# Splitting the picks' softmax, and the order of hits and high parts in the last retrieval head of a PEER block on one Trainium2 core

## The reference, cut to what matters

```
q = (xt @ w_query).reshape(T, PEER_HEADS, 2, D_HALF)
s = jnp.einsum('thpd,hpnd->thpn', q, sub_keys)
top_s, top_i = lax.top_k(s, PEER_TOPK)
cand = (top_s[:, :, 0, :, None] + top_s[:, :, 1, None, :]).reshape(T, PEER_HEADS, PEER_TOPK * PEER_TOPK)
best_s, best_c = lax.top_k(cand, PEER_TOPK)
i1 = jnp.take_along_axis(top_i[:, :, 0], best_c // PEER_TOPK, axis=-1)
i2 = jnp.take_along_axis(top_i[:, :, 1], best_c % PEER_TOPK, axis=-1)
ids = i1 * N_KEYS + i2
gates = jax.nn.softmax(best_s, axis=-1)
y[t] = sum_k gelu(expert_down[ids[t, k]] . x[t]) * gates[t, k] * expert_up[ids[t, k]]
```

## Time and profile before

| what | value |
|---|---|
| median of 3 runs | 1507.16 us (1506.37 to 1509.75) |
| the profiled execution, its own time | 1509.32 us |
| its span in the profile | 1507.5 us |
| mean granted TensorE clock | 0.993 |
| PE busy | 1453.1 us, 96% |
| DVE, ACT, POOL busy | 1162.8, 626.2 and 576.9 us |

### The profile page before, as it was taken

The page is one execution under the profiler, slowest core; times in us unless marked ns, Lnnn a source line. Parts: engine busy times, 40 slices in busy tenths (PEclk is TensorE's granted clock), DMA queues, the critical chain, the costliest instruction groups (busy, mean ns, idle before and its releaser), DMA issues.

```text
span 1507.5 us, 21376 instructions
## 1 busy us (share of the span) xinstructions
PE 1453.1 (96%) x7494; PEld 1252.9 (83%) x7494; DVE 1162.8 (77%) x2434; ACT 626.2 (42%) x985; POOL 576.9 (38%) x460
## 2 busy tenths in 40 slices
PE   3999999999999989999999999999999999999997
PEld 3455548999999889999988888888888888888886
DVE  6557565667888978988757787878778788888887
ACT  3134434344544357776633333333333333333334
POOL 0000011136444356888923343334334344444340
PEclk9999999999999999999999999999999999999999
DMA  9944303546464457787799999999999999999993
GB/s 350 387 176 168 99 28 119 156 140 228 132 204 168 127 177 255 266 286 266 256 377 372 336 341 360 351 336 340 362 331 358 344 362 340 339 383 348 331 334 108
DMA packets 186554, 404.89 MB, mean 269 GB/s; under 512 B 13064, under 2 KB 100688, under 8 KB 184784
## 3 DMA queue, kind: packets, MB, share of 16 engines
q1 hardware_dynamic: 146864, 243.86, 46.1%
q0 software_dynamic: 36864, 134.23, 24.2%
q10 hardware_dynamic: 2720, 25.44, 4.6%
HBM read 360.49 MB, written 42.99 MB: 268 GB/s over the span
## 4 chain that ended last, share of the span: by engine, by line
PE 87%; DVE 5%; POOL 3%; ACT 2%; issue 2%; DMA 2%; SPq 0%; POOLq 0%; ACTq 0%; DVEq 0%
PE bank L1838 11%; PE bank L1839 11%; PE bank L1840 11%; PE bank L1765 10%; PE bank L1767 10%; PE bank L1766 10%; PE bank L1820 4%; PE bank L1662 4%; PE bank L1707 3%; PE bank L1734 2%; PE bank L1735 2%; PE bank L1733 2%; PE bank L1646 2%; POOL gated L727 2%; PE bank L1755 1%
## 5 line engine op out<-in xcount | busy, mean ns | idle before, releaser
L1765 PE MATMUL bank<-h2hi,dhi 128*128 128x384 f32 x1024 | 348.1, 340 | 11.5 <-DVE dlo L1264 10.2
L1767 PE MATMUL bank<-h2hi,dlo 128*128 128x384 f32 x1024 | 344.7, 337 | 0.0
L1766 PE MATMUL bank<-h2lo,dhi 128*128 128x384 f32 x1024 | 344.3, 336 | 0.0
L1838 PE MATMUL bank<-uhi,ahi 128*128 128x512 f32 x768 | 299.6, 390 | 2.4 <-DVE alo L1489 2.4
L1264 DVE TENSOR_TENSOR dlo<-down,dhi 128x1024 fp32r<-128x1024 f32 x128 | 164.9, 1289 | 174.6 <-ACT dhi L856 167.5
L1839 PE MATMUL bank<-ulo,ahi 128*128 128x512 f32 x768 | 299.3, 390 | 0.0
L1840 PE MATMUL bank<-uhi,alo 128*128 128x512 f32 x768 | 299.2, 390 | 0.0
L680 POOL DMA_INDIRECT rows<-in_peer_up,ids x128 | 162.7, 1271 | 237.3 <-DVE y L1341 207.2
L680 POOL DMA_INDIRECT rows<-in_peer_down,ids x128 | 160.6, 1255 | 216.2 <-DVE rows L1332 197.4
L856 ACT ACTIVATE dhi<-down 128x1024 fp32r<-128x1024 f32 x128 | 135.1, 1056 | 216.3 <-PE bank L1767 208.7
L1765 PEld LDWEIGHTS bank<-h2hi,dhi 128*128 128x128 f32 x1024 | 193.4, 189 | 16.2 <-DVE dlo L1264 13.3
(11 more groups left out here) (201 smaller groups left out, 1935.2 us busy)
## 6 DMA issues: line engine op xcount, KB each, us to landing
down<-in_down_t SPq DMA_DIRECT2D x128, 512.0 KB
up<-in_peer_up SPq DMA_DIRECT2D x128, 512.0 KB
ada<-in_w_ada SPq DMA_DIRECT2D x48, 512.0 KB, 11.3
gate<-gates_dram SPq DMA_DIRECT2D x32, 768.0 KB, 9.1
gates_dram<-stage ACTq DMA_DIRECT2D x11, 2048.0 KB, 7.1
gel_dram<-gel SPq DMA_DIRECT2D x80, 192.0 KB
gelu<-gel_dram SPq DMA_DIRECT2D x80, 192.0 KB
wq<-in_peer_query SPq DMA_DIRECT2D x16, 512.0 KB, 5.3
```

What stands on the lines that cost most here:

```text
L1765: pe.matmul(bank[7 * s][:, 0:TD], dhi[s][:, k, :], h2hi[:, k, 0:TD], start=k == 0, stop=False)
L1766: pe.matmul(bank[7 * s][:, 0:TD], dhi[s][:, k, :], h2lo[:, k, 0:TD], start=False, stop=False)
L1767: last = pe.matmul(bank[7 * s][:, 0:TD], dlo[s][:, k, :], h2hi[:, k, 0:TD], start=False, stop=k == KT - 1)
L1838: pe.matmul(got[:], ahi[j][:, tokens], uhi[j][:, half], start=first, stop=False)
```

## The change

It does four things.

1. The softmax's subtraction and Exp are done in two parts: heads 0 to 6 (VectorE before the last head's `top16`, ScalarE right behind the last scores' copies), and head 7 alone (VectorE right behind `picks_of(7)`, ahead of low 46; ScalarE where Exp stood). `best_exp` is the new function on ScalarE, `best_sub` on VectorE.
2. ScalarE's hits of head 7 are cut into halves: half 0, then high 47 and Gelu 45, then half 1, then high 48 and Gelu 46.
3. GpSimd waits for `dve_half` of the last head before `weigh_hits(6)`, that is until the last head's sums are written.
4. VectorE does low 49 ahead of `select(7)` and not behind the numbers; low 50 comes ahead of the three row operations, low 51 behind hot rows 0, and low 52 stays behind hot rows 1.

```
@@ gpsimd
+            gp.wait_ge(dve_half, PH)
             for s in range(2):
                 weigh_hits(PH - 2, s)
             measure_hits(PH - 1)
@@ scalar
+            def hits_of(h, s):
+
+                flat = hit[s][:].rearrange("p b i j -> p (b i j)")
+                act.wait_ge(pool_off, 2 * h + s + 1)
+                act.activation(flat, flat, ACT.Abs).then_inc(act_far, 1)
+                act.wait_ge(act_far, 2 * h + s + 1)
+                act.activation(flat, flat, ACT.Relu, bias=ones[:, 0:1], scale=-1.0).then_inc(act_hit, 1)
+
             def hits(h):
-
                 for s in range(2):
...
+                    hits_of(h, s)
@@ scalar
+            def best_exp(heads):
+                act.activation(best[:, :, heads, :], pick[:, 2, :, heads, :], ACT.Exp).then_inc(act_gexp, 1)
+
@@ scalar, in the loop over heads
                 scores_of_out(h, (0, 1))
+                if h == PH - 1:
+                    act.wait_ge(dve_bsub, 1)
+                    best_exp(slice(0, PH - 1))
                 for n in range(a + 4, a + PER_HEAD):
                     early(n, n % 2)
@@ scalar
             for n in range(a + 2, a + 6):
                 early(n, n % 2)
-            act.wait_ge(dve_bsub, 1)
-            act.activation(best[:].rearrange("p b h k -> p (b h k)"),
-                           pick[:, 2].rearrange("p b h k -> p (b h k)"), ACT.Exp).then_inc(act_gexp, 1)
-            early(a + 6, (a + 6) % 2)
-            hits(PH - 1)
-            for n in range(a + 7, PICKS_G):
+            act.wait_ge(dve_bsub, 2)
+            best_exp(slice(PH - 1, PH))
+            for s in range(2):
+                hits_of(PH - 1, s)
+                early(a + 6 + s, (a + 6 + s) % 2)
+            for n in range(a + 8, PICKS_G):
                 early(n, n % 2)
@@ vector
+            def best_sub(heads):
+                wide = heads.stop - heads.start
+                first = best[:, :, heads, 0:1].broadcast_to([P, NB, wide, TOPK])
+                ve.tensor_tensor(pick[:, 2, :, heads, :], best[:, :, heads, :], first, ALU.subtract).then_inc(dve_bsub, 1)
+
             for h in range(PH):
                 last = h == PH - 1
+                if last:
+                    best_sub(slice(0, PH - 1))
@@ vector
+                if last:
+                    best_sub(slice(PH - 1, PH))
                 next_lo()
...
-            first = best[:, :, :, 0:1].broadcast_to([P, NB, PH, TOPK])
-            ve.tensor_tensor(pick[:, 2], best[:], first, ALU.subtract).then_inc(dve_bsub, 1)
             next_lo()
-            ve.wait_ge(act_gexp, 1)
+            ve.wait_ge(act_gexp, 2)
...
                              ALU.mult).then_inc(dve_pick, 1)
+            next_lo()
             next_lo()
             select(PH - 1)
@@ vector
             for u in range(2):
                 hot_rows(u, u)
-                next_lo()
+                if u == 0:
+                    next_lo()
```

## The result

Six runs of the changed kernel have a median of 1498.53 us (1496.19 to 1501.51), six of the kernel before beside them 1507.38; the ratio is 0.9941, 95% interval 0.9923 to 0.9958. The profiled execution took 1501.51 us, its span is 1499.6: 7.9 less than before.

What follows compares the result with a forecast made beforehand. PE, busy 96% of the span, bounds the kernel, so only its gaps and slow-clock stretches count. Terms -1.0 - 0.3 - 2.65 - 1.6 - 0.95 + 1.05 sum to -5.4 us: median 1507.16 to 1501.8, range 1499.4 to 1506.0.

Steps and rivals of the forecast that it cites:

- tile 43: Last head: with low 42 and the sums undisturbed, PE starts this tile at 517.73 instead of 518.74, -1.0 us.
- clock in tile 48: Last head: with the gap ahead of it down to 1.1 us, the slow stretch in this tile goes, -1.6 us.
- wait ahead of the gates: First gate turn: PE waits for GpSimd's hot rows, +1.05 us, bounds 0 and +2.6.
- the table loads cost their 1.28: Rival on ScalarE: close table loads hold ACT longer than their rows, tile 48 ends 2 us later, total -3.4; chance 0.04.
- the clock in tile 48 was full: Rival in the last head: the low clock stays, +1.6 us and a few tenths, total -3.6; chance 0.16.
- GpSimd did not take the gain at the gates: Rival at the gates: GpSimd's list takes 13.5 us for 12.36 and PE waits, total only -2; chance 0.13.
- tile 48 ended early: Slower rival: tile 48 ends later than about 550.5, delaying the row operations queued behind low 50, 1510.4 us; chance 0.05.
- the gaps did not move to another place: Rival in the last head: gaps are moved, not removed, and the change does nothing, 1507 us; chance 0.07.
- ahead of 47: Last head: PE's gap ahead of tile 47 is 1.1 us for 1.27 and its restart, -0.3 us.
- ahead of 48: Last head: PE's gap ahead of tile 48 is 1.1 us for 3.75, -2.65 us.
- ahead of 50 and 51: Tail: the gap ahead of tile 50 goes and one of 0.5 us stands ahead of tile 51, -0.95 us.
- Behind the gates' first turn nothing changes: Gate turns after the first and the rest of the kernel: no gain or loss, 0 us in the sum.

Runs made afterwards that it cites:

- e1: The changed kernel without GpSimd's wait for the last sums before it weighs hits 6: 1502.17 us, ratio to the kernel before 0.9960.
- e7: The changed kernel with one gated row of eight on GpSimd instead of two, and three one-hot rows on ScalarE instead of two: 1497.88 us.
- e10: The kernel before with e7's edit (one gated row on GpSimd, three one-hot rows on ScalarE): 1505.58 us.
- e5: The changed kernel again, nothing altered, for a second profile: 1499.55 us against 1505.45 for the kernel before, ratio 0.9960.
- e13: The kernel before, unchanged, for a third profile: one time, 1506.28 us.
- e14: The changed kernel, unaltered, for a third profile: one time, 1501.31 us.
- e2: The kernel before plus only GpSimd's wait for the last sums: 1506.66 us, ratio 0.9995.
- e3: The changed kernel, but ScalarE does high 47 and Gelu 45 first, then both halves of hits 7: 1504.73 us, ratio to the kernel before 0.9984.
- e16: The same kernel as e3 (hits 7 whole), for a second profile: one time, 1505.35 us.
- e9: The kernel before, unchanged, for a second profile: 1508.06 us.
- e11: The same kernel as e7, run again on the same chip as e10: 1498.81 us.
- e12: The changed kernel with an extra down tile ahead of the transposes, other reorderings and e7's edit: 1493.79 us, ratio to the kernel before 0.9914.

## Why the prediction was wrong

**What held.** The place and the mechanism: low 42 and the sums undisturbed (1.20 and 0.60), tile 43 without a gap (taken back alone by e1, 1.1 to 1.3), the gap ahead of 41 and its clock untouched, the clock in tile 48 full (-1.6), low 47 and 48 each waiting out a product, the short wait ahead of the gates. Its five rivals are out: the table loads cost their 1.28, the clock in tile 48 was full, GpSimd did not take the gain at the gates, tile 48 ended early, and the gaps did not move to another place.

The Trainium skill, page ScalarE: Activation LUTs, section What ACT_TABLE_LOAD costs, has about 2.66 us for each switch, a load and a drain. The rows of all four switches disagree: each load starts within 0.02 us of the end of the instruction before it, takes 1.28, and the next instruction starts within 0.02 us behind it.

**What was mis-sized**, in the sum's own terms:

| term | forecast | measured |
|---|---|---|
| tile 43 | -1.0 | -1.2 |
| ahead of 47 | -0.3 | -0.6 |
| ahead of 48 | -2.65 | -2.9 |
| clock in tile 48 | -1.6 | -1.6 |
| ahead of 50 and 51 | -0.95 | -1.1 |
| wait ahead of the gates | +1.05 | +0.4 |
| sum | -5.4 | -7.0 |

The measured column is from the starts of the tiles in the two timelines. The 1.6 us are five terms that all erred to the same side, and the largest is the wait ahead of the gates, 0.65. Its list on GpSimd, the gathers and hot rows, took 10.55 us (551.82 to 562.37) where the prediction went by 12.36 and took 11.3. It also started 0.6 earlier counted from tile 41 (42.97 for 43.57), while PE came to the gates 0.5 earlier. The second step is the products of hits 7: the first started 0.4 earlier against the clock than I had carried it (532.67 is 23.8 behind tile 41, I had 531.95 - 507.73 = 24.2), the second ended 0.5 earlier, and a low part that waits for a product ends 1.1 behind it, so both gaps were 0.6 and not 1.1. The tail was nearly right: tile 51 starts 4.47 behind tile 50, where an undisturbed tile takes 4.16, so a small part of its gap is still there.

**The other step that failed** is "Behind the gates' first turn nothing changes". The time behind it changes from one execution to the next, by the number of waits in the gates and by the clock behind the gap for `alo`. Between the two kernels, in the mean of three profiles each, the gate turns from the second on are 1.2 us shorter (172.4 for 171.2), as one full wait less would make them, and the part behind the gates 0.8 (760.0 for 759.2), of which 0.4 is the shorter wait for `alo`. From tile 41 to the second gate turn the same mean is 6.9 shorter; the pair with the edit of e7 is 6.8 apart in the medians and only 5.8 in its profiles, since the profile of e10 has the full clock in tile 48. Three profiles of each do not show that the change makes the waits rarer, nor that it doesn't. The first set of runs gave 8.85 between the kernels, the second 5.9 (e5), the single pair e13 and e14 5.0. What of the 8.85 beyond 7.0 is the change's stays open.

**The range** failed with these two steps. Its lower end stood on a bound of -7 and half a microsecond for the runs, while the count of waits alone moves a run by up to 6 (184.44 in e1 for 178.17), and by 3.6 in the kernel before. The three runs of before that it went by are 3.4 apart, 1.7 to either side, and not 1.4. And its bounds for the wait, 0 and +2.6, give -6.45 and -3.85, not the -7 and -4.2 that it used; that the stretch then came out at -7.0 does not bear them out.

## What to carry to other kernels

Where two engines wait for each other instruction by instruction, read which of one engine's instructions are not held up (here MAX8 and its kin) and put the other engine's long ones beside those; it cost one wait on a semaphore. Take a stretch from one marked instruction to another and compare stretches, not spans: here it repeats to 0.15 us while spans of one kernel differ by 4. Look at the granted clock in it too: in e10 the full clock in tile 48 alone took 1.5 us off it. When every gap in a row is predicted by the same carried clock, the errors add up on one side, and the range should hold that sum.

## What the runs showed of the hardware that was not expected

- The low clock behind a gap of PE is not set by the gap's length alone. Tile 48 behind a gap of 3.49 to 3.51 took 5.84 (three profiles of before), 6.74 (e2) and 4.30 (e10), at 0.86, 0.78 and 1.00 of the full clock in the window; behind 2.72 it took 5.83 (e3, e16). In one and the same kernel, before, the gap for `alo` of 2.37 was followed by a window at 0.86 and that of 2.36, in e9, by one at 1.00.
- VectorE's one-hot rows and GpSimd's gated rows in the gates fall together in two ways. In an undisturbed turn of the changed kernel a pair of GpSimd's rows takes 1.70 us; in the turns ahead of the one wait it takes 2.75, then 3.58, 2.90 and 3.20, until PE has to wait:

```profile
616.09 0.97 POOL L725 COPY own<-pickT 128x6 f32<-128x6 f32 x1 [0.60 <-PE bank L1839]
617.23 2.75 POOL L728 TENSOR_SCALAR gated<-iota,own 128x128 f32<-128x128 f32 x2 [0.17 <-POOL own L725]
619.94 0.18 POOL L725 COPY own<-pickT 128x6 f32<-128x6 f32 x1
620.29 3.58 POOL L728 TENSOR_SCALAR gated<-iota,own 128x128 f32<-128x128 f32 x2 [0.17 <-POOL own L725]
...
633.31 1.16 PE L1839 MATMUL bank<-gated,onehot 128*128 128x128 f32 x8 [0.91 <-POOL gated L728]
```

  With one row on GpSimd in place of two, none of four profiles (e7, e10, e11, e12) had such a wait, and the 24 turns took 178.17 us in each.
